# Four smaller pieces a bit in the selection, early block sums on VectorE, one weighted sum for the requests' index

## The chip, the cores and the metric

The kernel runs on one core of a Trainium2 chip. Its time is the device time of the whole program in microseconds. The kernel before took 1695.43 us, the median of three runs (1693.01 to 1697.52). All data are fp32.

## The reference

A trunk of two layers serves a prompt of 1024 tokens and eight later requests ("samples") of 16 tokens each, with caches of 512 tokens, with the same weights. Per layer: RMSNorm, one projection to the inputs of four branches of attention (A, B, C, M), the branches, each multiplied by silu of its own gate columns, and an output projection of 1024x1024 that is added to the stream. Branch A is the one that matters here: an indexer scores every key, and each query attends only to its top k.

```python
def dsa_attend(q, qi, wi, lim, k, v, ki, topk):
    L = k.shape[1]
    dots = jnp.einsum('bqhd,bld->bqhl', qi.astype(F32), ki.astype(F32)) * D_IDX ** -0.5
    score = jnp.einsum('bqh,bqhl->bql', wi.astype(F32) * H_IDX ** -0.5, jax.nn.relu(dots))
    admissible = jnp.arange(L)[None, :] < lim[:, None]
    score = jnp.where(admissible[None], score, -jnp.inf)
    top_s, top_i = lax.top_k(score, topk)
...
def merge(p, o_a, o_b, o_c, o_m, w_o):
    parts = [o.reshape(lead + (-1,)) * jax.nn.silu(p[g])
             for o, g in ((o_a, 'a_g'), (o_b, 'b_g'), (o_c, 'c_g'), (o_m, 'm_g'))]
    return jnp.concatenate(parts, axis=-1) @ w_o
```

## The kernel before, in words

**Order.** `program_order()` writes one list of steps for the whole program; every engine walks the list and does its own share of each step, in order, with semaphores between the engines. So the place of a step in the list is its place in each engine's queue. A tile is 128 tokens: eight of the prompt and a ninth (`ST_`) with the samples. The projection runs in chunks of 512 weight columns (A1, mm, B1, B2, C1, C2, M1, A2, then O0 and O1 for the output). A unit is one chunk for one tile: `project(c, t)` emits its matmuls in parts (`Pp`, then `P`), and between the parts the steps of an attention pack: `S` (scores on TensorE), `L` (logits on VectorE, exponentials on ACT), `T` (transposes), `Z` (the scaling of the gate), `V` (values, and the product with the gate on VectorE). A pack with several heads has two `L` and `T` halves; the second ones come from `odd_heads()`, just before the unit's `P`. TensorE writes scores to two buffers in psS, transposes to two in psT, and projections and values to two in psX.

**Selection.** The k-th largest score of each query is found bit by bit. VectorE keeps a threshold per strip (seven strips of 384 to 1024 scores, `thr`), and for each of 32 bits `count_below` counts the scores under the threshold (line 1572, one instruction and a read of its accumulator per strip); step `bit` updates the threshold from the counts (lines 1748 to 1758) and counts the strips `FIRST` (tiles 7, 6, 3), step `rest` the strips `REST` (samples, 5, 4, 2). Each ends in a drain. Then `equals`, `ranks` and `mask` make a mask of each strip. `select(time)` doles these steps out: it adds `time` to an account and emits steps, at planned costs, while the account is positive. A unit has two such places (four where two packs go through a unit, `two_packs`): at the start, and before `P`. All steps must be out before branch A's first pack.

**The requests' index.** For the samples, step `is` j scores a pair of requests (TensorE to psS, relu on ACT into one of two work buffers), and `iw` sums two such pairs over the heads with weights `wsel`: matmuls on line 1202 into a quarter of 32 rows per pair, then a copy and an addition on VectorE (lines 1736, 1737). `iw` 0 stands within the unit B1 `ST_`, `iw` 2 behind the unit B1 0, right before the first bit.

**Output projection.** It takes seven block products instead of eight (a Strassen scheme) per pair of tiles p and chunk: steps `G` c p n on TensorE (line 1142), each followed by additions to the stream on VectorE (line 1663, `ADDED_TO`) that free psX. The blocks need sums first: `Tw`, four sums of weight quarters of 128x1024 per chunk (line 1991), and `Sh`, four sums of rows of 128x512 per pair p (line 2008). All are made by GpSimd. `Tw` O0 and `Sh` 0 and 1 are emitted in one piece, four or eight at once, in the units of A2, when what they overwrite is free.

**Branch A's end.** In A2 units VectorE does the rotation of the queries (lines 1552 to 1558), the gate product (1652), the branch product (`V`, 1866) and, once, the product of the gathered samples with their gate (`R`, 1872), which frees a psT buffer.

Of the kernel before, what the change touches and what calls it, by code (L numbers as in the profile page):

```python
# [74 lines left out]
FIRST, REST = [NT - 1, NT - 2, 3], [ST_, 5, 4, 2]  # L75
# [67 lines left out]
def topk_steps():  # L143


    out = [(kind, i) for i in range(32) for kind in ("bit", "rest")]
    return out + [("bit", 32)] + [(kind, t) for t in [ST_] + SEL_TILES for kind in ("equals", "ranks", "mask")]


def program_order():  # L150
# [11 lines left out]
    queue = []  # L162

    def emit(*s, ahead=0):
# [3 lines left out]
    cost = lambda x: {"bit": 0.5 + count(FIRST) * (x[1] < 32), "rest": count(REST)}.get(  # L168
        x[0], {"equals": 1.9, "ranks": 2.2, "mask": 2.4}.get(x[0], 0) * STRIP_L.get(x[1], 0) / 960 + 0.5)
# [117 lines left out]
    for l in range(DEPTH):  # L287
# [54 lines left out]
        emit("iw", 0)  # L342
# [14 lines left out]
        units += [("M1", t) for t in [ST_] + TILES[:NT]] + [("A2", t) for t in A2_ORDER]  # L357
        for c, t in units:
# [252 lines left out]
def encoder(nc, d):  # L611
# [3 lines left out]
    with ExitStack() as ctx:  # L615
# [155 lines left out]
        n_work = {u: n for n, u in enumerate(steps("ip", "is"))}  # L771
        qs_ready = Signal(sem("qs_ready"), [(l, s) for l, s in order if s[0] == "is" or (s[0] == "S" and is_sample(s[1]))])
# [28 lines left out]
        rows_combined = Signal(sem("rows_combined"), events(["Sh"], lambda s: s[1:]))  # L801
        w_combined = Signal(sem("weights_combined"), events(["Tw"], lambda s: s[1:]))
# [21 lines left out]
        def row_sum(p, i):  # L824
# [7 lines left out]
                    (s4, upper[:, LAST_LINES, :], s2, ALU.subtract)][i]  # L832

# [184 lines left out]
        def _(pe):  # L1018
# [16 lines left out]
            for l, s in order:  # L1035
# [81 lines left out]
                elif k == "G":  # L1117
# [7 lines left out]
                    if (p, n) == (0, 2):  # L1125
                        pe.wait_ge(*w_combined.on((c, 3)))
                    if c == "O0" and n >= 3:
                        pe.wait_ge(*rows_combined.on((p, max(n - 3, 1))))
# [64 lines left out]
                elif k == "iw":  # L1193

                    both = [s[1], s[1] + 1]
                    for j in both:
# [3 lines left out]
                    for c0, c1 in ((0, PAST), (PAST, SKEYS)):  # L1200
                        for j in both:
                            mm = pe.matmul(S.ap(s)[32 * j:32 * j + 32, c0:c1], wsel[:, j, :],
                                           buf(n_work[l, ("is", j)] % 2)[:, c0:c1], start=True, stop=True)
# [138 lines left out]
        def _(act):  # L1342
# [4 lines left out]
            for l, s in order:  # L1347
# [135 lines left out]
                elif k in ("ip", "is"):  # L1483
# [3 lines left out]
                    if n >= 2:  # L1487
# [4 lines left out]
                        else:  # L1492
                            use = ("iw", pv[1] // 2 * 2)
                            act.wait_ge(*S.fill(use, pl).on(use, pl))
                    nc.scalar.activation(buf(n % 2)[:, 0:L], S.ap(s)[:, 0:L], ACT.Relu).then_inc(S.empty(s).sem, 1)  # L1495
# [37 lines left out]
        def _(dve):  # L1533
# [42 lines left out]
            for l, s in order:  # L1576
# [51 lines left out]
                elif k == "P" and (l, s[1:]) in worked.upto:  # L1628
# [24 lines left out]
                    dve.drain().then_inc(worked.sem, 1)  # L1653
                elif k == "G":
# [74 lines left out]
                elif k == "iw":  # L1729
                    j = s[1]  # L1730
                    dve.wait_ge(*S.fill(s).on(s))
                    if j == 0:
                        dve.wait_ge(*tmask.on("m"))
                    r0 = slice(32 * j, 32 * j + 64)
                    dst = sc[r0, SC_OFF[ST_]:SC_OFF[ST_] + SKEYS]
                    v.tensor_copy(dst[:, 0:PAST], S.ap(s)[r0, 0:PAST])
                    v.tensor_tensor(dst[:, PAST:SKEYS], S.ap(s)[r0, PAST:SKEYS], dst[:, PAST:SKEYS], ALU.add
                                    ).then_inc(S.empty(s).sem, 1)
                    dve.drain().then_inc(scored.sem, 1)
                elif k == "K" and s[1][0] == "bit":  # L1740
# [19 lines left out]
                    if i < 32:  # L1760
                        count_below(FIRST)
                        dve.drain()
                elif k == "K" and s[1][0] == "rest":
                    count_below(REST)
# [111 lines left out]
        def _(pool):  # L1876
# [89 lines left out]
            for l, s in order:  # L1966
# [9 lines left out]
                if k == "Tw":  # L1976

                    c, i = s[1:]
                    if i == 0:
                        pool.wait_ge(*w_loaded[chunks.index((l, c)) % 2].on(c))  # L1980
                        if c == "O0":
                            last_m = [q for ql, q in packs if ql == l and q[0] == "M"][-1]
                            for use in (("V", last_m), ("V", last_sample["A"])):
                                pool.wait_ge(*X.fill(use).on(use))
                        else:
                            pool.wait_ge(*logits.on((packs_of("A", 5)[-1], 1)))
                    t1, t2, t3, t4 = w_sums[c]
                    b11, b12 = [w_quarter(c, FIRST_LINES, h) for h in range(2)]
                    b21, b22 = [w_quarter(c, LAST_LINES, h) for h in range(2)]
                    out, a, b = [(t1, b12, b11), (t3, b22, b12), (t2, b22, t1), (t4, b21, t2)][i]  # L1990
                    g.tensor_tensor(out, a, b, ALU.subtract).then_inc(w_combined.sem, 1)
                    pool.drain()
                elif k == "Sh":

                    p, i = s[1:]
                    if i == 0:
                        if p >= 2:
                            use = ("G", "O1", p - 2, 6)
                            pool.wait_ge(*X.fill(use).on(use))
                        else:  # L2000
                            pool.wait_ge(*gated.on("A"))
                            pool.wait_ge(*k_stored.on("mm"))
                            pool.wait_ge(*v_stored.on(("mm", 1)))
                            pool.wait_ge(*sm_stored.on("s"))
# [4 lines left out]
                    pool.drain().then_inc(rows_combined.sem, 1)  # L2009
# [276 lines left out]
```

## Time and profile before

| | |
|---|---|
| median of three runs | 1695.43 us |
| profiled execution | 1695.91 us, its span 1694.1 us |
| TensorE matmul, weight load | 1657.6 us (98%), 1116.2 us (66%) |
| VectorE | 1083.6 us (64%) |
| ACT | 626.7 us (37%) |
| GpSimd | 321.7 us (19%) |
| mean granted clock of TensorE | 0.997 |

Shares are of the span. Both layers run the same steps, one layer behind the other. The views quoted below have, in their rows, the engine (PE is TensorE, DVE VectorE, POOL GpSimd), the line of the kernel and the operation. Engines overlap, so busy times don't add up to the span; a busy time of TensorE is modelled, with some overlap of neighbouring groups.

### The profile page before, as it was taken

The page shows a single profiled execution, that of the slowest core. Times are in us where ns is not written, and L with a number is a line of the kernel's source. Part 1 is how long each engine was busy: PE and PEld are TensorE (multiplying, and loading weights), DVE is VectorE, ACT ScalarE, POOL GpSimd, SP SyncE. Part 2 cuts the span into 40 slices and gives each one's busy share as a digit, 9 for nine tenths or more (in the row PEclk, how much of TensorE's full clock was granted, in tenths as well). Part 3 has the DMA queues.
Part 4 walks back from the last instruction along what each step waited for, and adds up shares of the span by engine and source line. Part 5 has one row for each costly group of instructions (what it writes and reads, how often), then busy time and mean ns, then how long its engine had stood idle before and what let it go on. Part 6 is the DMA issues. An engine that isn't in the chain of part 4 may idle for free.

```text
span 1694.1 us, 28367 instructions
## 1 busy us (share of the span) xinstructions
PE 1657.6 (98%) x9815; PEld 1116.2 (66%) x9815; DVE 1083.6 (64%) x2829; ACT 626.7 (37%) x1509; POOL 321.7 (19%) x500
## 2 busy tenths in 40 slices
PE   9999999999999999999999999999999999999998
PEld 4466666766677755588754666666666777556885
DVE  5747888788877334455445288887888773354454
ACT  3532334333343444422134323343333434445221
POOL 2242321100001022223021423220000010223110
PEclk9999999999999999999999999999999999999999
DMA  9343324123222341112251523241233132412021
GB/s 341 150 172 97 128 94 144 42 78 107 91 86 97 112 120 37 69 38 88 99 175 51 166 83 129 91 144 41 78 110 103 71 122 97 117 31 82 1 100 62
DMA packets 46382, 171.32 MB, mean 101 GB/s; under 512 B 11473, under 2 KB 11953, under 8 KB 43041
## 3 DMA queue, kind: packets, MB, share of 16 engines
q1 hardware_dynamic: 29632, 130.68, 22.8%
q0 software_dynamic: 16608, 38.83, 7.0%
q8 instruction: 80, 1.31, 0.3%
q14 instruction: 62, 0.50, 0.1%
HBM read 141.83 MB, written 30.73 MB: 102 GB/s over the span
## 4 chain that ended last, share of the span: by engine, by line
PE 63%; DVE 27%; issue 4%; ACT 3%; ACTq 1%; DVEq 1%; DMA 1%
PE psX L1113 32%; DVE lower L1572 15%; PE psX L1142 11%; PE psT L1026 6%; PE psX L1317 5%; PE psS L1250 4%; DVE work L1834 4%; PE psS L1169 2%; ACTq L1463 1%; DVE gate L1652 1%; PE psX L1026 1%; DVE work L1832 1%; ACT work L1504 1%; ACT gate L1377 1%; DVE gate L1848 1%
## 5 line engine op out<-in xcount | busy, mean ns | idle before, releaser
L1113 PE MATMUL psX<-wring,hT 128*128 128x512 f32 (+2 forms) x1504 | 609.5, 548 | 4.2 <-ACT qT L1423 2.6
L1113 PEld LDWEIGHTS psX<-wring,hT 128*128 128x128 f32 x1504 | 272.4, 191 | 222.4 <-issue 214.3
L1572 DVE TENSOR_SCALAR_CACHE_REDUCE lower<-sc,thr 128x640 uint8<-128x640 f32 (+5 forms) x462 | 407.3, 933 | 16.9 <-issue 9.0
L1113 PE MATMUL psX<-hT,wring 128*128 128x256 f32 (+1 forms) x1600 | 328.3, 359 | 4.5 <-ACT gate L1462 3.6
L1504 ACT ACTIVATE work<-work,stat 128x256 f32<-128x256 f32 (+7 forms) x288 | 200.0, 695 | 315.9 <-DVEq L1837 313.1
L1113 PEld LDWEIGHTS psX<-hT,wring 128*128 128x128 f32 x1600 | 274.2, 190 | 37.3 <-issue 8.2
L1513 ACT COPY work<-psT 128x512 f32<-128x512 f32 (+2 forms) x352 | 157.3, 488 | 295.2 <-PE psT L1026 292.8
L1026 PEld LDWEIGHTS psT<-con,work 128*128 128x128 f32 x1080 | 121.9, 141 | 77.0 <-issue 54.7
L1026 PE MATMUL psT<-con,work 128*128 128x128 f32 x1080 | 160.1, 279 | 10.9 <-DVE bias L1872 7.1
L1834 DVE CUSTOM_DVE_ANT_0 work<-psS,bias 128x640 f32<-128x640 f32 (+7 forms) x120 | 86.2, 718 | 39.1 <-issue 23.7
L1882 POOL DMA_DIRECT2D scratch_oscr<-gate x54 | 30.7, 569 | 346.2 <-DVEq L1868 294.3
L1834 DVE CUSTOM_DVE_ANT_0 work<-psS,sc 128x384 f32<-128x384 f32 (+5 forms) x48 | 42.8, 891 | 43.7 <-PE psT L1026 38.3
L1250 PE MATMUL psS<-kv,qT 64*128 64x512 f32 (+3 forms) x384 | 69.9, 482 | 0.0
L1317 PE MATMUL psX<-work,kv 128*64 128x128 f32 x1056 | 68.2, 277 | 0.0
L1317 PEld LDWEIGHTS psX<-work,kv 128*64 128x64 f32 x1056 | 56.7, 137 | 12.8 <-issue 12.3
L1495 ACT ACTIVATE work<-psS 128x640 f32<-128x640 f32 (+5 forms) x56 | 41.9, 748 | 61.2 <-PE psS L1191 28.2
L1142 PE MATMUL psX<-wring,hT 128*128 128x256 f32 x256 | 58.1, 380 | 0.0
L1663 DVE TENSOR_TENSOR kv<-psX,kv 128x256 f32<-128x256 f32 (+1 forms) x70 | 36.9, 535 | 32.5 <-PE psX L1142 31.7
L1663 DVE TENSOR_TENSOR xr<-psX,xr 128x256 f32<-128x256 f32 (+1 forms) x70 | 36.9, 535 | 30.7 <-PE psX L1142 29.9
L1866 DVE TENSOR_TENSOR gate<-psX,gate 128x256 f32<-128x256 f32 (+1 forms) x64 | 22.9, 358 | 50.0 <-ACTq L1521 41.7
L1504 ACT ACTIVATION_READ_ACCUMULATOR work<-work,stat 128x1 f32 x288 | 53.7, 187 | 0.0
L1552 DVE TENSOR_TENSOR lower<-stage,con 128x48 f32<-128x48 f32 (+1 forms) x36 | 10.8, 300 | 65.8 <-ACTq L1463 64.9
(272 smaller groups left out, 1953.8 us busy)
## 6 DMA issues: line engine op xcount, KB each, us to landing
wring<-in_w SPq DMA_DIRECT2D x16, 2048.0 KB, 8.5
cache<-in_kB SPq DMA_DIRECT2D x16, 512.0 KB, 6.1
cache<-in_vB SPq DMA_DIRECT2D x16, 512.0 KB, 4.0
cache<-in_kC SPq DMA_DIRECT2D x16, 512.0 KB, 6.1
cache<-in_vC SPq DMA_DIRECT2D x16, 512.0 KB, 4.8
scratch_oscr<-gate POOLq DMA_DIRECT2D x54, 128.0 KB, 2.0
hT<-scratch_oscr SPq DMA_DIRECT2D x18, 384.0 KB, 3.0
kv<-in_x SPq DMA_DIRECT2D x9, 512.0 KB, 6.1
```

The source lines that it names most:

```text
L1026: return pe.transpose(out, src, ident)
L1113: mm = pe.matmul(out, lhs, rhs, start=(kt == 0), stop=(kt == KT - 1))
L1142: mm = pe.matmul(X.ap(s)[:, 0:W], lhs[:, kt, :], rhs[:, kt, :], start=(kt == 0), stop=(kt == KT // 2 - 1))
L1169: mm = pe.matmul(S.ap(u)[:, c0:c1], qT[half, h // 2, t * P:(t + 1) * P], kA[half, 0, c0:c1], start=True, stop=True)
L1250: mm = pe.matmul(S.ap((s, hp))[:, at + c0:at + c1], q[half, :], keys[half, k0 + c0:k0 + c1], start=True, stop=True)
L1317: mm = pe.matmul(o[64 * hp:64 * hp + 64, i // 2 * P:(i // 2 + 1) * P], v, turned_buf(hp)[:, at:at + P], start=(b == 0), stop=(b == len(kb) ...
L1495: nc.scalar.activation(buf(n % 2)[:, 0:L], S.ap(s)[:, 0:L], ACT.Relu).then_inc(S.empty(s).sem, 1)
L1504: nc.scalar.activation(x, x, ACT.Exp, scale=-1.0, bias=stats(p)[:, 0, i:i + 1], accum_out=stats(p)[:, 1, i:i + 1]).then_inc(probs.sem, 1)
L1513: nc.scalar.copy(turned_buf(hp)[:, 512 * g:512 * g + w], T.ap(u)[:, 0:w]).then_inc(T.empty(u).sem, 1)
L1572: v.tensor_scalar(lower[:, at:at + STRIP_L[t]], sc[:, o], thr[:, n:n + 1], 0.0, ALU.is_lt, ALU.add, accum_out=below[:, n:n + 1])
L1663: last = v.tensor_tensor(x, X.ap(s)[:, 0:W].unsqueeze(1).to_broadcast([P, c1 - c0, W]), x, ALU.add)
L1834: last = v.tensor_tensor_reduce(dst, src, b_, -1.0, -NEG, ALU.add, ALU.min, nm)
```

## The change

It does three things. First, the counts of a bit go in four steps instead of two (`COUNTED`: tiles 7 and 2 with the update, then 6 and 3, then 5 and the samples, then 4), and `project` has four places for them in every unit, each worth a quarter of the pace: in a unit without two packs these are at the start, behind `operands()`, before `P`, and behind `P`. Second, `Tw` O0 and `Sh` 0 and 1 are VectorE's, and they are emitted from a list `sums`, two at a time at two places of a unit and one behind each `G` step. `Tw` O1 and `Sh` 2 and 3 stay on GpSimd; `Tw` O1 gets a wait more. Third, `iw` is one step for all four pairs, behind the unit B1 0; relu for pairs 2 and 3 writes into rows of `gate` instead of the work buffers, for which ACT waits for norm 10.

```diff
-FIRST, REST = [NT - 1, NT - 2, 3], [ST_, 5, 4, 2]
+COUNTED = [[7, 2], [6, 3], [5, ST_], [4]]
...
-    out = [(kind, i) for i in range(32) for kind in ("bit", "rest")]
+    out = [(kind, i) for i in range(32) for kind in ("bit", "second", "third", "fourth")]
...
+    sums = []
+
+    def add_sums(n):
+        for _ in range(n):
+            if sums:
+                emit(*sums.pop(0))
...
-        time = pace[0] / (4 if two_packs else 2)
+        time = pace[0] / 4
...
             odd_heads()
             select(time)
+            add_sums(2)
             emit("Pp", c, t, 3, 4)
...
             emit("Pp", c, t, 0, 2)
             operands()
+            select(time)
             emit("Pp", c, t, 2, 5)
         odd_heads()
         select(time)
+        add_sums(2)
         emit("P", c, t)
+        if not two_packs:
+            select(time)
...
-        emit("iw", 0)
...
-                emit("iw", 2)
+                emit("iw")
...
-                if c == "A2" and due and (l, (kind, at, 0)) not in o:
-                    for i in range(4):
-                        emit(kind, at, i)
+                if c == "A2" and due and (kind, at) not in begun:
+                    begun.append((kind, at))
+                    sums.extend((kind, at, i) for i in range(4))
...
             for n in range(7):
                 emit("G", c, p, n)
+                add_sums(1)
...
+            if s[0] == "is" and s[1] >= 2:
+                return gate[:, 4 * s[1] - 8:4 * s[1] - 4, :].rearrange("p a b -> p (a b)")
+            return buf(n_work[l, s] % 2)
...
-                    both = [s[1], s[1] + 1]
-                    for j in both:
+                    for j in range(PAIRS):
                         pe.wait_ge(*relued.on(("is", j)))
                     pe.wait_ge(*scored.on(("wsel",)))
                     scores_free(s)
                     for c0, c1 in ((0, PAST), (PAST, SKEYS)):
-                        for j in both:
+                        for j in range(PAIRS):
...
+                elif k == "Tw" and s[1] == "O0":
+
+                    c, i = s[1:]
+                    if i == 0:
+                        dve.wait_ge(*w_loaded[chunks.index((l, c)) % 2].on(c))
+                    v.tensor_tensor(*w_sum(c, i), ALU.subtract)
+                    dve.drain().then_inc(w_combined[True].sem, 1)
+                elif k == "Sh" and s[1] < 2:
+
+                    p, i = s[1:]
+                    if i == 0:
+                        dve.wait_ge(*k_stored.on("mm"))
+                        dve.wait_ge(*v_stored.on(("mm", 1)))
+                        dve.wait_ge(*sm_stored.on("s"))
+                        for t in (2 * p, 2 * p + 1):
+                            dve.wait_ge(*o_loaded[t].on("o"))
+                    v.tensor_tensor(*row_sum(p, i))
+                    dve.drain().then_inc(rows_combined[True].sem, 1)
...
-                    count_below(REST)
+                elif k == "K" and s[1][0] in ("second", "third", "fourth"):
+                    count_below(COUNTED[("second", "third", "fourth").index(s[1][0]) + 1])
                     dve.drain()
...
-                if k == "Tw":
+                if k == "Tw" and s[1] == "O1":
...
-                elif k == "Sh":
+                elif k == "Sh" and s[1] >= 2:
```

## Rows read from the trace of the kernel before

**Rows 1.** The page, busy time of each engine, share of the span, instructions

```profile
PE 1657.6 (98%) x9815; PEld 1116.2 (66%) x9815; DVE 1083.6 (64%) x2829; ACT 626.7 (37%) x1509; POOL 321.7 (19%) x500
```

**Rows 2.** TensorE's waits: for whom, total us, times, longest

```profile
PE psT L1026 <- DVE bias L1872: 7.1, 2, 3.5
...
PE psT L1026 <- DVE gate L1872: 3.3, 4, 1.3
```

**Rows 3.** Busy us by stretch: four with bit rounds, and one behind

```profile
sum 400.00, PE 392.23 PEld 265.53 DVE 346.51 ACT 141.62 POOL 73.33; mean PE 98.06 PEld 66.38 DVE 86.63 ACT 35.41 POOL 18.33
...
255.00:345.00 90.00, 90.00 (x564) 62.27 (x564) 71.16 (x179) 34.22 (x76) 12.97 (x24) 1.00 0.25 87
```

**Rows 4.** VectorE's waits from 150 to 255 us, first row

```profile
DVE work L1834 <- issue: 5.4, 22, 0.7
```

**Rows 5.** Busy us from 640 to 720 and from 1480 to 1560, sum

```profile
sum 160.00, PE 152.04 PEld 88.33 DVE 72.30 ACT 78.23 POOL 39.46; mean PE 76.02 PEld 44.16 DVE 36.15 ACT 39.12 POOL 19.73
```

**Rows 6.** The timeline, 673 to 680 us: start, us, engine, line, operation

```profile
673.36 2.35 POOL L1991 TENSOR_TENSOR qT<-wring,qT 128x1024 f32<-128x1024 f32 x1 [0.16 <-issue]
673.78 1.97 DVE L1552 TENSOR_TENSOR lower<-stage,con 128x32 f32<-128x32 f32 x1 [1.89 <-ACTq L1463]
...
675.87 2.40 POOL L1991 TENSOR_TENSOR cache<-wring,qT 128x1024 f32<-128x1024 f32 x1 [0.16 <-issue]
...
676.15 2.17 DVE L1557 TENSOR_TENSOR stage<-stage,lower 128x32 f32<-128x32 f32 x1
...
678.25 0.18 DVE L1558 TENSOR_TENSOR stage<-stage,lower 128x32 f32<-128x32 f32 x1
...
679.50 0.42 DVE L1872 TENSOR_TENSOR bias<-psT,bias 128x256 f32<-128x256 f32 x1
...
679.99 0.47 PE L1026 MATMUL psT<-con,work 128*128 128x128 f32 x1 [3.52 <-DVE bias L1872]
```

**Rows 7.** Two stretches of low granted clock (PEclk)

```profile
679.20:686.10 6.90, 6.12 (x11) 2.94 (x12) 2.75 (x6) 1.83 (x5) 5.07 (x4) 0.51 0.01 2
1522.30:1525.70 3.40, 3.40 (x9) 1.82 (x7) 1.55 (x3) 1.38 (x4) 3.04 (x3) 0.50 0.00 0
```

**Rows 8.** VectorE's groups by line and form: count | busy us, mean ns

```profile
L1663 DVE TENSOR_TENSOR xr<-psX,xr 128x512 f32<-128x512 f32 x30 | 20.4, 686 | 12.0 <-PE psX L1142 11.9
...
L1565 DVE TENSOR_TENSOR hT<-hT,con 128x1024 f32<-128x1024 f32 x9 | 11.0, 1225 | 10.0 <-DMA hT<-in_xT 6.0 <-DMA con<-in_const 3.1
```

**Rows 9.** The timeline, layer 1's first G steps

```profile
1560.96 2.36 POOL L1991 TENSOR_TENSOR cache<-wring 128x1024 f32<-128x1024 f32 x1 [27.52 <-DMA wring<-in_w]
...
1566.16 1.89 PE L1142 MATMUL psX<-cache,hT 128*128 128x256 f32 x8
```

**Rows 10.** The timeline: half an index sum, and matmuls on four quarters

```profile
132.24 1.27 PE L1202 MATMUL psS<-work,wsel 128*32 128x512 f32 x8
...
155.12 1.07 PE L1226 MATMUL psS<-cache,qs 128*32 128x512 f32 x8
...
156.00 0.40 PE L1231 MATMUL psS<-kv,qs 128*32 128x128 f32 x8
```

**Rows 11.** The timeline, 162 to 165 us: counts within and across steps

```profile
162.73 1.14 DVE L1572 TENSOR_SCALAR_CACHE_REDUCE lower<-sc,thr 128x896 uint8<-128x896 f32 x1
...
163.79 0.74 DVE L1572 TENSOR_SCALAR_CACHE_REDUCE lower<-sc,thr 128x512 uint8<-128x512 f32 x1
...
164.63 0.88 DVE L1572 TENSOR_SCALAR_CACHE_REDUCE lower<-sc,thr 128x640 uint8<-128x640 f32 x1
```

**Rows 12.** Line 1572 alone by stretch: busy us (xinstructions)

```profile
150.00:255.00 105.00, 61.75 (x140) 1.00 0.32 106
...
1192.00:1292.00 100.00, 58.59 (x132) 1.00 0.27 93
```

**Rows 13.** The timeline, 197 to 198.5 us

```profile
197.42 0.35 ACT L1458 COPY kv<-psX 128x256 f32<-128x256 f32 x1
...
198.48 1.75 PE L1113 MATMUL psX<-hT,wring 128*128 128x256 f32 x7 [1.12 <-ACT gate L1462]
```

More of the change, by code:

```diff
@@ L167, in program_order @@
     count = lambda part: sum(STRIP_L[t] / 960 + 0.25 for t in part)
-    cost = lambda x: {"bit": 0.5 + count(FIRST) * (x[1] < 32), "rest": count(REST)}.get(
-        x[0], {"equals": 1.9, "ranks": 2.2, "mask": 2.4}.get(x[0], 0) * STRIP_L.get(x[1], 0) / 960 + 0.5)
+    cost = lambda x: {"bit": 0.5 + count(COUNTED[0]) * (x[1] < 32), "second": count(COUNTED[1]), "third": count(COUNTED[2]),
+                      "fourth": count(COUNTED[3])}.get(x[0], {"equals": 1.9, "ranks": 2.2, "mask": 2.4}.get(x[0], 0) * STRIP_L.get(x[1], 0) / 960 + 0.5)
     def select(time):
@@ L800, in encoder @@
         o_loaded = [Signal(sem(f"branch_tile{t}_loaded"), each("o"), lambda e: 16) for t in TILES]
-        rows_combined = Signal(sem("rows_combined"), events(["Sh"], lambda s: s[1:]))
-        w_combined = Signal(sem("weights_combined"), events(["Tw"], lambda s: s[1:]))
+        early = lambda u: u[1][1] in ("O0", 0, 1)
+        sums_of = lambda kind, by_dve: [(l, s[1:]) for l, s in steps(kind) if early((l, s)) == by_dve]
+        rows_combined = {b: Signal(sem(f"rows_combined{int(b)}"), sums_of("Sh", b)) for b in (True, False)}
+        w_combined = {b: Signal(sem(f"weights_combined{int(b)}"), sums_of("Tw", b)) for b in (True, False)}
         res_added = Signal(sem("residual_added"), outs)
@@ L832, in row_sum, with w_sum @@
                     (s4, upper[:, LAST_LINES, :], s2, ALU.subtract)][i]
+        def w_sum(c, i):
+            t1, t2, t3, t4 = w_sums[c]
+            b11, b12 = [w_quarter(c, FIRST_LINES, h) for h in range(2)]
+            b21, b22 = [w_quarter(c, LAST_LINES, h) for h in range(2)]
+            return [(t1, b12, b11), (t3, b22, b12), (t2, b22, t1), (t4, b21, t2)][i]
         def w_quarter(c, rows_, half):
@@ L1200, in _ @@
                     for c0, c1 in ((0, PAST), (PAST, SKEYS)):
-                        for j in both:
+                        for j in range(PAIRS):
                             mm = pe.matmul(S.ap(s)[32 * j:32 * j + 32, c0:c1], wsel[:, j, :],
-                                           buf(n_work[l, ("is", j)] % 2)[:, c0:c1], start=True, stop=True)
+                                           index_buf(l, ("is", j))[:, c0:c1], start=True, stop=True)
                     mm.then_inc(S.fill(s).sem, 1)
@@ L1486, in _ @@
                     act.wait_ge(*S.fill(s).on(s))
-                    if n >= 2:
+                    if k == "is" and s[1] >= 2:
+                        act.wait_ge(*normed.on(10))
+                    elif n >= 2:
                         pl, pv = [x for x in n_work if n_work[x] == n - 2][0]
@@ L1492, in _ @@
                         else:
-                            use = ("iw", pv[1] // 2 * 2)
-                            act.wait_ge(*S.fill(use, pl).on(use, pl))
-                    nc.scalar.activation(buf(n % 2)[:, 0:L], S.ap(s)[:, 0:L], ACT.Relu).then_inc(S.empty(s).sem, 1)
+                            act.wait_ge(*S.fill(("iw",), pl).on(("iw",), pl))
+                    nc.scalar.activation(index_buf(l, s)[:, 0:L], S.ap(s)[:, 0:L], ACT.Relu).then_inc(S.empty(s).sem, 1)
                     act.drain().then_inc(relued.sem, 1)
@@ L1760, in _ @@
                     if i < 32:
-                        count_below(FIRST)
+                        count_below(COUNTED[0])
                         dve.drain()
-                elif k == "K" and s[1][0] == "rest":
-                    count_below(REST)
+                elif k == "K" and s[1][0] in ("second", "third", "fourth"):
+                    count_below(COUNTED[("second", "third", "fourth").index(s[1][0]) + 1])
                     dve.drain()
@@ L1980, in _ @@
                         pool.wait_ge(*w_loaded[chunks.index((l, c)) % 2].on(c))
[L1981 to L1991, printed above, removed]
+                        pool.wait_ge(*X.fill(("V", last_sample["A"])).on(("V", last_sample["A"])))
+                        pool.wait_ge(*logits.on((packs_of("A", 5)[-1], 1)))
+                    g.tensor_tensor(*w_sum(c, i), ALU.subtract).then_inc(w_combined[False].sem, 1)
                     pool.drain()
-                elif k == "Sh":
+                elif k == "Sh" and s[1] >= 2:
                     p, i = s[1:]
                     if i == 0:
[L1997 to L2004, printed above, removed]
+                        use = ("G", "O1", p - 2, 6)
+                        pool.wait_ge(*X.fill(use).on(use))
                         for t in (2 * p, 2 * p + 1):
@@ L2008, in _ @@
                     g.tensor_tensor(*row_sum(p, i))
-                    pool.drain().then_inc(rows_combined.sem, 1)
+                    pool.drain().then_inc(rows_combined[False].sem, 1)
                 elif k == "G" and s[3] == 6:
```

17 lines of the change are left out of this document (8 added, 9 removed).

## The prediction

> **What bounds the kernel now.** I read the page first: the reader is to see TensorE busy for 98% of the span and VectorE for 64% [rows 1]. A busy TensorE can hide stalls, so next come the waits by engine. The longest in TensorE's list are two waits of 3.5 us, 7.1 us together, for line 1872 on VectorE, the product of branch A's sample rows with their gate [rows 2]. Then the stages: in four stretches of 95 to 105 us, where the bit rounds of the selection lie beside attention, TensorE is busy for 392.2 of 400 us and VectorE for 346.5 [rows 3]. In the first of them the head of VectorE's list of waits is its own issue: it never waits for data [rows 4]. So two engines run at nearly one rate there, and what is added to VectorE can reach TensorE. Elsewhere VectorE has room: it is busy for 72.3 of 160 us in the two stages where branch A meets the output projection [rows 5]. TensorE bounds the kernel; a change pays where it takes a stall or work from TensorE.
>
> **Part 1: the early sums move from GpSimd to VectorE.** Before, GpSimd makes four sums of 1024 columns (2.35 and 2.40 us in the rows) for O0 and eight of 512 for row pairs 0 and 1, per layer. The timeline shows what they do to VectorE. The rotation products of 128x32 on lines 1552 and 1557, like the one on line 1558 at 0.18 us, take 1.97 and 2.17 us, and each of the two ends when a GpSimd sum ends (675.75 beside 675.71; 678.32 beside 678.27). The two slow ones stand before line 1872 in VectorE's queue; it starts at 679.50, and TensorE's next transpose at 679.99, after 3.52 us idle [rows 6]. Without the two delays (1.79 + 1.99 = 3.8 us) line 1872 would start near 675.7, and the idle would end where it began, at 676.5. I take it as gone in both layers: -7.0 us.
> At this gap the granted clock falls: 0.51 for 6.9 us from 679.2, and 0.50 for 3.4 us from 1522.3, where the same wait ends in the second layer [rows 7]. That is 1.2 GHz instead of 2.4, right behind TensorE's longest idle time. Half of both is lost: (6.9 + 3.4) / 2 = 5.1 us. With the gap gone I take it as kept: -5.1 us (0 if the clock falls all the same).
> The sums cost VectorE 4 x 1.22 + 8 x 0.69 = 10.4 us a layer, by its products of 1024 and additions of 512 columns [rows 8]. Eight of a layer's twelve stand, two at a time, in the units A2 6 and 7, where VectorE is idle more than half the time [rows 5]; a pair of 1.22 delays a branch product by at most 2.6 us ahead of idle of that size: zero. If that cover were gone, up to 10.4 us a layer would be paid.
> The other four, of row pair 1, now stand behind the first four G steps. In layer 1 GpSimd's four sums for O1 run there one behind the other, the first from 1560.96 and 2.36 us long, so for some 9.5 us [rows 9]. The moved sums have both inputs in SBUF, as the slow products of [rows 6] have, so each but the first may wait for up to 2.35 us, and the additions that free psX queue behind. TensorE has two psX halves and 1.9 us of work a step [rows 9], so a good part is hidden: 0 to 7 us, I take +2.5, nearer the hidden end.
> The Trainium skill has the cause: SBUF — State Buffer, "SBUF: two separate sides", says that VectorE with two SBUF inputs and GpSimd take a shared port pair exclusively, for the whole instruction. It speaks for the -7.0 and against the G steps of layer 1; by it that collision could be the full 7, and the sum 4.5 us later.
>
> **Part 2: one weighted sum.** Each half of the requests' index takes TensorE 1.27 us: four matmuls of 512 and four of 128 columns, on two of four column quarters. Eight matmuls of 512 on all four quarters take 0.88 us (155.12 to 156.00) and eight of 128 take 0.40 [rows 10], so all four pairs fit into the time of one half. One half a layer goes, 1.2 us with the overlap: -2.4 us (0 at worst: a matmul group is not longer than before). VectorE saves a copy and an addition a layer. Relu for pairs 2 and 3 writes into gate rows; the wait added to ACT there is for a norm long done, and behind it nothing is late. The selection begins where it did.
>
> **Part 3: four pieces a bit.** The seven strips and the planned pace stay. A unit has four places instead of two, but places one and two have nothing of VectorE's between them, so ahead of a unit's second logits pass stand on average the same counts as before. New is that the unit's gate product (line 1652) comes before the last piece, and that pieces end at finer steps. Each piece ends in a drain. Inside a piece the count of 512 follows the start of that of 896 by 1.06 us (1.14 long); at its end the next piece's count follows the start of the 512 by 0.84 us (0.74 long) [rows 11]. A boundary costs 0.10 + 0.08 = 0.18 us. There are two more a bit: 32 x 2 x 2 = 128, 23 us of VectorE. Each bit shows as 14 instructions of line 1572 (seven counts, seven reads); the four stretches hold 531, from 140 in the first to 132 in the last [rows 12], 38 bits: 13.7 us where VectorE never waits.
> How much reaches TensorE? It waited 8.2 us in these stretches, ten rows of the kind shown, 0.6 to 1.1 us each as a rule. In that one ACT can't empty psX until its exponentials are through, and they wait for VectorE's logits, behind three counts; TensorE stands 1.12 us [rows 13]. Best, finer pieces take all 8.2 away; worst, all 23 pass. Behind a stretch VectorE has room again, busy for 71.2 of 90 us from 255 [rows 3], so a growing lag may be carried out of it. I take 7 passing and 5 of the waits gained: +2.
> The Trainium skill, VectorE: DVE Perf Modes, "The DRAIN you can't avoid", says that a flush stands behind each operation anyway and a semaphore adds nothing; by it the split would be free and only the gain of 5 would stand. The 0.18 us of the rows speaks against it for an explicit drain behind a count.
>
> **Sum,** against the profiled execution's 1695.9 us (span 1694.1 and 1.8 around it): 1695.9 - 7.0 - 5.1 + 2.5 - 2.4 + 2 = 1685.9. The median of the runs shown is 0.5 lower, 1695.4, so I forecast 1685.5. A difference under 0.3% (5 us) can't be told from none.
>
> **Rivals.** (a) The split is free or a gain: 6 of TensorE's 8.2 us of waits go and the collision is hidden: 1695.4 - 14.5 - 6 = 1675 (1672 to 1679). For it: the waits are short against a piece; against: the boundary's 0.18.
> (b) The gap stays under another name: line 1872 is still behind a rotation and a branch product, half the gap and half the lost clock remain: 1695.4 - 6 - 2.4 + 4.5 = 1691.5. For it: TensorE waits for line 1872 in four other places, 3.3 us [rows 2]; against: delays of 3.8 us fill the 3.5.
> (c) The split doesn't do what it says, because places one and two adjoin on VectorE: finer pieces win none of the waits and cost the 7: 1695.4 - 12.1 - 2.4 + 2.5 + 7 = 1690.4.
> (d) Slower: the boundaries. If VectorE is the true bound wherever bits are counted, all 23 us reach TensorE: 1695.4 - 14.5 + 23 = 1704. It turns the change to a loss from 14.5/128 = 0.11 us passed on per boundary. Against it: VectorE's room behind the stretches.
>
> **Chances.** Forecast 0.56 (its own range 1680 to 1690), (a) 0.16, (b) 0.10, (c) 0.10, (d) 0.08. Faster by over 0.3%: the first two and a third of (b) and (c), 0.78; within: 0.14; slower: 0.08. The range leaves out the low end of (a) and most of (d): 1675 to 1694.
>
> **What would show it.** TensorE's wait for line 1872 at the end of branch A gone in both layers, the clock 1.00 there, lines 1552 and 1557 never over 0.5 us: part 1. In layer 1's first G steps TensorE waiting for line 1663, and a moved sum of over 1 us: the collision. Two groups on line 1202 instead of four: part 2. TensorE's waits in the four stretches, 8.2 before, about 10 after: part 3. I am wrong if that stands at under 4 or over 20, or if the clock falls elsewhere.

## The result, and the profile after

The changed kernel takes 1721.2 us (median of 4 runs, 1720.7 to 1723.4) beside 1696.0 us for the kernel before on the same chip: ratio 1.0152, 95% interval 1.0140 to 1.0164. It is 25 us slower, where the forecast was 10 us faster; the time lies outside the range and beyond the slower rival's 1704.

The page of the changed kernel first: busy time of each engine, beside [rows 1].

```profile
PE 1661.1 (96%) x9815; PEld 1116.2 (65%) x9815; DVE 1103.4 (64%) x2849; ACT 625.1 (36%) x1509; POOL 281.9 (16%) x476
```

TensorE is busy for 3.5 us more in a span that is 27.5 us longer (1721.6 against 1694.1), so nearly all of the loss is waiting. TensorE's waits over the whole span (for whom, total, times, longest) say on whom:

```profile
PE psX L1053 <- ACTq L1542: 18.2, 14, 2.5
PE psX L1140 <- ACT kv L1451: 8.2, 4, 2.9
PE psT L1053 <- DVE gate L1914: 7.8, 4, 2.3
...
PE psX L1140 <- DMA wring<-in_w: 3.0, 2, 1.9
```

The first row of [rows 2], 7.1 us for the sample rows' product of branch A, is gone. In its place stands ScalarE: it copies the transposes out of psT late (up to line 1542) and empties psX late (line 1451). In the stretches of the selection the waits are these (133 to 600 us, then 975 to 1440 us):

```profile
PE psX L1053 <- ACTq L1542: 8.1, 5, 2.5
PE psX L1140 <- ACT kv L1451: 4.0, 2, 2.5
PE psT L1053 <- DVE gate L1914: 3.9, 2, 2.3
PE psX L1140 <- ACT qT L1449: 2.8, 2, 1.5
PE psX L1140 <- ACT gate L1456: 0.4, 1, 0.4
PE psX L1140 <- ACT gate L1488: 0.4, 1, 0.4
...
PE psX L1053 <- ACTq L1542: 8.2, 5, 2.5
PE psX L1140 <- ACT kv L1451: 4.2, 2, 2.9
```

With the rows left out they sum to 19.6 + 19.6 = 39.2 us; the same view of the kernel before sums to 7.3 + 6.7 = 14.0. In the four stretches of [rows 3], each moved by the lag of its work, the 8.2 us of the forecast are about 19 (4.8, 5.8, 2.9 and 5.7), so its sign of being wrong, over 20, did not quite show; the larger part of the growth lies outside them. ScalarE is busy for a third of the span, so it is late because it is itself held up. VectorE's waits in the changed kernel show by what:

```profile
DVE lower L1579 <- ACTq L1489: 57.6, 30, 6.8
DVE gate L1679 <- ACTq L1489: 54.2, 25, 9.5
```

Line 1679 is the gate product of step P (1652 before), and line 1489 the end of ScalarE's copies and gates out of psX. Before, VectorE waited 31.5 us there, 16 of them in two waits of 8 ahead of the selection, which stay. So VectorE waits for ScalarE's work on psX, and ScalarE, in order too, waits for VectorE's logits. The experiments below take this apart.

The granted clock, as in [rows 7], by windows (the column ahead of the last two):

```profile
117.00:120.40 3.40, 3.40 (x5) 1.35 (x4) 3.28 (x3) 0.00 (x0) 0.00 (x0) 0.51 0.06 25
181.90:185.30 3.40, 3.40 (x5) 1.32 (x6) 2.41 (x6) 0.41 (x1) 2.92 (x6) 0.50 0.94 320
543.70:547.10 3.40, 3.40 (x25) 2.24 (x20) 0.59 (x2) 0.37 (x1) 0.60 (x1) 0.50 0.02 5
1035.20:1038.60 3.40, 3.40 (x6) 1.34 (x5) 2.63 (x8) 0.82 (x2) 3.06 (x6) 0.51 0.68 247
1397.10:1400.50 3.40, 3.40 (x16) 2.34 (x13) 1.02 (x4) 0.74 (x2) 0.60 (x1) 0.50 0.11 39
```

The two places of before run at the full 2.4 GHz; instead there are five stretches at 1.2 GHz, each close behind an idle time of TensorE of 1.9 to 2.9 us. TensorE is busy throughout, so half of 17.0 us is lost, 8.5, against 4.8 before (half of the 9.5 us busy in [rows 7]). This sign of being wrong, the clock falling elsewhere, did show.

The end of branch A, on VectorE's timeline, beside [rows 6]:

```profile
693.13 0.19 DVE L1584 TENSOR_TENSOR stage<-stage,lower 128x32 f32<-128x32 f32 x1
693.24 0.19 DVE L1585 TENSOR_TENSOR stage<-stage,lower 128x32 f32<-128x32 f32 x1
...
694.51 0.42 DVE L1914 TENSOR_TENSOR bias<-psT,bias 128x256 f32<-128x256 f32 x1
```

The rotation step that took 2.17 us takes 0.19, and the product comes 1.4 us behind it. This part of the forecast holds.

Where the time went follows from when the same products start in the two traces. In each layer the lag grows by 16.1 and 16.8 us during the selection (32.9). Of that the added waits are 39.2 - 14.0 = 25.2, and four of the five slow stretches 6.8. It falls by 5.9 and 4.3 us at the end of branch A, falls by 1.3 in each layer where half of the index sum is gone, and grows by 1.9 and 0.9 right behind that, by 1.8 for the first slow stretch, and by 1.8 in layer 1's G steps. With 0.5 us at the start that is 32.9 - 10.2 - 2.6 + 2.8 + 1.8 + 1.8 + 0.5 = 27.0 of the 27.5 us.

### The profile page after: what moved, and what is told of

It reads as the page before. It is cut to its first block, busy times and chain, and to the rows that moved or that the text cites. A ratio compares the mean times of both kernels' runs of the same rounds, so it can differ in the third digit from the quotient of the medians.

```text
span 1721.6 us, 28477 instructions
## 1 busy us (share of the span) xinstructions
PE 1661.1 (96%) x9815; PEld 1116.2 (65%) x9815; DVE 1103.4 (64%) x2849; ACT 625.1 (36%) x1509; POOL 281.9 (16%) x476
## 4 chain that ended last, share of the span: by engine, by line
PE 57%; DVE 30%; issue 5%; ACT 3%; ACTq 2%; DVEq 2%; DMA 1%
PE psX L1140 30%; DVE lower L1599 16%; PE psX L1169 10%; PE psT L1053 5%; DVE work L1876 5%; PE psX L1343 4%; PE psS L1276 4%; PE psS L1196 2%; ACTq L1489 1%; DMA wring<-in_w 1%; ACT work L1531 1%; DVE gate L1679 1%; PE psX L1053 1%; DVE gate L1890 1%; ACT gate L1403 1%
## 5 line engine op out<-in xcount | busy, mean ns | idle before, releaser
L1599 DVE TENSOR_SCALAR_CACHE_REDUCE lower<-sc,thr 128x640 uint8<-128x640 f32 (+5 forms) x462 | 417.4, 935 | 33.8 <-issue 16.5
L1053 PE MATMUL psT<-con,work 128*128 128x128 f32 x1080 | 159.8, 279 | 10.1 <-DVE gate L1914 7.8
L1679 DVE SCALAR_TENSOR_TENSOR gate<-stage,gate 128x256 f32<-128x256 f32 (+1 forms) x46 | 21.7, 472 | 55.9 <-ACTq L1489 54.2
L1874 DVE TENSOR_SCALAR_CACHE_REDUCE work<-psS 128x256 f32<-128x256 f32 x72 | 30.6, 425 | 35.2 <-PE psT L1053 25.0
```

The source lines that it names most:

```text
L1053: return pe.transpose(out, src, ident)
L1599: v.tensor_scalar(lower[:, at:at + STRIP_L[t]], sc[:, o], thr[:, n:n + 1], 0.0, ALU.is_lt, ALU.add, accum_out=below[:, n:n + 1])
L1679: v.scalar_tensor_tensor(out=ga, in0=th, scalar=1.0, in1=ga, op0=ALU.add, op1=ALU.mult)
```

## The experiments

**One part at a time.** Part 3 alone, on the kernel before:

```diff
-FIRST, REST = [NT - 1, NT - 2, 3], [ST_, 5, 4, 2]
+COUNTED = [[7, 2], [6, 3], [5, ST_], [4]]
...
-        time = pace[0] / (4 if two_packs else 2)
+        time = pace[0] / 4
...
             operands()
+            select(time)
             emit("Pp", c, t, 2, 5)
...
         emit("P", c, t)
+        if not two_packs:
+            select(time)
```

> The kernel before with part 3 alone: four pieces a bit at four places. The recorded forecast's steps give +2 us (7 passing, 5 of waits gained), its rival of boundaries at most +23. Theory 1 (each added boundary costs VectorE about 0.24 us and all of it reaches TensorE) and theory 2 (the places put bit and second piece ahead of the second logits pass) together: about +33 us, ratio 1.019, with TensorE waiting over 8 us for the evacuation of psX in the V packs. If this stands under +10, the loss of the changed kernel is an interaction with the moved sums.

It is 35.0 us slower (1731.2 against 1696.2; ratio 1.0209, 1.0193 to 1.0224), near the 33 of the two theories together. The loss is part 3's own. Part 1 alone, with this as its core:

```diff
+                elif k == "Tw" and s[1] == "O0":
+                    ...
+                    v.tensor_tensor(*w_sum(c, i), ALU.subtract)
+                    dve.drain().then_inc(w_combined[True].sem, 1)
+                elif k == "Sh" and s[1] < 2:
+                    ...
+                    v.tensor_tensor(*row_sum(p, i))
```

> The kernel before with part 1 alone: the early sums on VectorE, two pieces a bit. The recorded forecast's steps give -7.0 - 5.1 + 2.5 = -9.6 us, with the clock at 1.00 at the end of branch A and waits for line 1663 in layer 1's first G steps. The two traces' offsets give -6.4 in layer 0 and -4.3 in layer 1, +1.8 for the collision, and the lost clock kept: about -9 to -12. If it is within 3 us of before, the gain was handed back by something the offsets hide.

It is 6.5 us faster (1689.7; 0.9960, 0.9947 to 0.9973), less than the 9 to 12 expected. Between the traces the end of branch A gives 5.7 and 4.6 us, and layer 1's G steps take 1.9 back; 1.7 us are lost before the first branch product, where the two kernels do the same: up to there the executions of the several kernels lie from 1.0 us ahead of the kernel before to 1.6 behind it. Parts 1 and 2 together, the counts as before:

```diff
-        emit("iw", 0)
...
-                emit("iw", 2)
+                emit("iw")
```

> Parts 1 and 2 together, the counts as before. The recorded forecast's steps give -7.0 - 5.1 + 2.5 - 2.4 = -12 us, 1684. The offsets between the traces of before and after give for part 2 a gain of 1.2 us a layer, and behind it a wait for the next weight block's DMA (1.9 and 0.9 us) and a half clock of 3.4 us in the first layer: about 0 to +1 in all, so 1688 to 1690 by them.

It is 6.3 us faster (1689.2 against 1695.5; 0.9968, 0.9954 to 0.9983), as part 1 alone: part 2 brings no gain that the runs can tell. The timeline of this kernel shows it, where TensorE comes 1.2 us earlier to the next weight block:

```profile
114.92 2.84 PE L1136 MATMUL psX<-wring,hT 128*128 128x512 f32 x6 [1.36 <-DMA wring<-in_w]
```

With part 1 alone it starts at 114.75 in the trace of that kernel with one drain less, without a wait. The sum saved only brings TensorE to a transfer that has not landed: its waits for the weight blocks are 2.6 us in two places, against 0.3 with part 1 alone, and the sum saved is 2.4.

**Part 3 in two: pieces, and places.** Four pieces at the two old places, then two pieces at the four new places (each is one half of the first diff above):

> The kernel before with four pieces a bit, but still two places in every unit, so two more drains a bit (128 in all). Theory 1 (boundaries): nearly the whole of part 3's loss, +20 to +30 us. Theory 2 (placement): under +8. The recorded forecast's price (0.18 us a boundary, 7 of 23 passing): +2 to +7.

> The kernel before with two pieces a bit, but four places in every unit, each worth a quarter of the pace: no more drains than before, only other positions for the steps. Theory 1: no loss, within 3 us. Theory 2: most of part 3's loss, +15 or more, with waits of TensorE for the evacuation of psX by ScalarE.

The pieces cost 12.7 us (1708.9; 1.0075, 1.0060 to 1.0090), the places 27.6 (1723.8; 1.0170, 1.0153 to 1.0188). The pieces' loss lies between the 20 to 30 of theory 1 and the 2 to 7 of the forecast's price. Theory 1 (boundaries are the loss) fails as the main cause, and my guess in the forecast that the places do no harm fails outright. Theory 2 has the size, but not the reason: by the program order the counts ahead of a unit's second logits pass are of 2432 scores a query in each of the 21 units that have such a pass in the selection, in the kernel before and with the four places alike. First the pieces: VectorE's count group with four pieces, then with four places but two pieces (busy, mean ns, idle before).

```profile
L1573 DVE TENSOR_SCALAR_CACHE_REDUCE lower<-sc,thr 128x640 uint8<-128x640 f32 (+5 forms) x462 | 417.4, 935 | 32.5 <-issue 16.6
```

```profile
L1575 DVE TENSOR_SCALAR_CACHE_REDUCE lower<-sc,thr 128x640 uint8<-128x640 f32 (+5 forms) x462 | 407.3, 933 | 17.2 <-issue 7.9
```

The kernel before has 407.3 and 16.9. So 128 boundaries cost VectorE 10.1 + 15.6 = 25.7 us, 0.20 each. That half of it reaches the end is not shown, because the pieces also regroup the strips. Ahead of the second logits pass, where 2432 scores a query stood in each unit, there are now from 1408 to 3456 (2444 on average). In an early unit with 2816 (four counts instead of three) TensorE waits 2.64 us for ScalarE to empty psX, and a slow stretch follows. VectorE is 1.2 us later there than in the kernel before at the first logits pass and 1.9 at the second (TensorE was 0.6 us ahead of it until then), so the boundaries so far and the larger counts both have a share. TensorE's lag grows by 4.2 us there, and by 3.9 in the same unit of layer 1, 1.3 and 0.9 of which are given back. That is 5.9 of the 12.7 us in two units, and TensorE's waits for this copy (line 1451 of the changed kernel) are 7.2 us with the pieces alone, 1.4 before and 1.4 with the places alone. What the drains and what the regrouping cost was not separated. Then the places: VectorE's waits with two pieces at four places.

```profile
DVE gate L1655 <- ACTq L1466: 66.8, 30, 8.2
```

31.5 us have become 66.8. One of them on that kernel's timeline, VectorE and ScalarE:

```profile
1095.07 0.83 DVE L1837 CUSTOM_DVE_ANT_0 work<-psS,bias 128x640 f32<-128x640 f32 x1 [0.18 <-issue]
...
1097.79 0.42 DVE L1655 SCALAR_TENSOR_TENSOR gate<-stage,gate 128x256 f32<-128x256 f32 x1 [1.89 <-ACTq L1466]
1098.35 0.88 DVE L1575 TENSOR_SCALAR_CACHE_REDUCE lower<-sc,thr 128x640 uint8<-128x640 f32 x1
```

```profile
1095.98 0.83 ACT L1507 ACTIVATE work<-work,stat 128x640 f32<-128x640 f32 x1 [4.01 <-DVEq L1840]
...
1096.81 0.35 ACT L1461 COPY kv<-psX 128x256 f32<-128x256 f32 x1
1097.06 0.38 ACT L1464 ACTIVATE stage<-psX 128x256 f32<-128x256 f32 x1
1097.34 0.38 ACT L1465 ACTIVATE gate<-psX 128x256 f32<-128x256 f32 x1
```

The same unit in the kernel before, VectorE and then ScalarE's last copy out of psX:

```profile
1080.42 0.82 DVE L1834 CUSTOM_DVE_ANT_0 work<-psS,bias 128x640 f32<-128x640 f32 x1 [0.18 <-issue]
...
1081.40 0.88 DVE L1572 TENSOR_SCALAR_CACHE_REDUCE lower<-sc,thr 128x640 uint8<-128x640 f32 x1 [0.15 <-issue]
...
1083.94 0.61 DVE L1572 TENSOR_SCALAR_CACHE_REDUCE lower<-sc,thr 128x384 uint8<-128x384 f32 x1
...
1084.64 0.43 DVE L1652 SCALAR_TENSOR_TENSOR gate<-stage,gate 128x256 f32<-128x256 f32 x1
```

```profile
1082.69 0.39 ACT L1462 ACTIVATE gate<-psX 128x256 f32<-128x256 f32 x1
```

The second logits pass (1095.07) releases ScalarE's exponentials (1095.98), behind them ScalarE empties psX (1096.81 to 1097.72), and only then the gate product of P can run (1097.79). In the kernel before the `rest` counts stand between the logits and P (1081.40 to 1084.55) and fill this time: ScalarE is through at 1083.08, and P starts without a wait. With the fourth place they stand behind P: VectorE idles for 1.89 us and then counts for 3.2 us ahead of this unit's branch product and the next unit's logits. From 1074 to 1160 us this idle time is 0.4 us before and 7.9 us here, and TensorE's lag grows by 5.6 us from 1053 to 1155 us of the kernel before (13.3 to 18.9). The planner's program order tells how often: behind P stand 2 of a layer's 64 steps with counts before, 14 of 64 here (15 with the last update of the threshold), and 29 of 128 in the changed kernel.

**Is it the fourth place?** The place added behind `operands()` against the one behind P, each alone, two pieces a bit:

```diff
-        time = pace[0] / (4 if two_packs else 2)
+        time = pace[0] / 4
         select(time)
...
             operands()
+            select(time)
...
-        select(time)
+        select(time if two_packs else 2 * time)
         emit("P", c, t)
```

> The kernel before with two pieces a bit and three places in a unit: the second place is there, the fourth (behind the unit's gate product P) is not. The first four runs gave a new theory 3: VectorE, which works in order, meets P before counts that stood ahead of it, and sits idle until ScalarE has emptied the unit's last projection (its waits for ScalarE at the gate product 31.5 us before, 66.8 with the four places). Theory 3: no loss here, within 3 us, and that wait stays near 31. Theory 2 in its first form (counts ahead of the second logits pass): ten steps of each layer move from the first place to the second, with nothing of VectorE's between, so it too gives no change; what it can't give is a gain. If this loses over 8 us, theory 3 isn't the cause of the 27.6.

```diff
         odd_heads()
-        select(time)
+        select(time if two_packs else time / 2)
         emit("P", c, t)
+        if not two_packs:
+            select(time / 2)
```

> The kernel before with two pieces a bit, the second place left out and the fourth kept (weights 1/2, 1/8, 1/8 and 1/4). Behind P stand 15 steps a layer, as with all four places (2 before). Theory 3: the whole loss of the four places, +22 to +30 us, with VectorE waiting 60 us or more for ScalarE at the gate product. Rival (the second place harms): within 5 us of before.

The second of these edits gives half of the pace to the first place, a quarter to the one before P and a quarter to the one behind it; the weights that its expectation names are not those of the edit. Without the fourth place the time is that of before (1696.0 against 1696.4; 0.9997, 0.9988 to 1.0006). With it and not the second the whole loss is there (1723.6; 1.0159, 1.0144 to 1.0174). VectorE's wait in the one and in the other:

```profile
DVE gate L1653 <- ACTq L1464: 31.5, 15, 8.2
```

```profile
DVE gate L1654 <- ACTq L1465: 65.9, 29, 7.9
```

And the changed kernel itself without its fourth place, whose share of the pace goes to the third:

```diff
-        select(time)
+        select(time if two_packs else 2 * time)
         add_sums(2)
         emit("P", c, t)
-        if not two_packs:
-            select(time)
```

> The changed kernel with one edit undone: no fourth place behind the unit's gate product, its share of the pace goes to the third; four pieces a bit and parts 1 and 2 stay. Theory 3: the loss of the fourth place goes (places_134 lost 27.2 us and pieces and places together 35.0 where the pieces alone lost 12.7, so 22 to 27): 1721.2 - 22 to 27 = 1694 to 1699, and VectorE's wait for ScalarE at the gate product falls from 54 to about 30 us. If the four pieces themselves were the loss (the recorded rival of the boundaries), it stays over 1712.

It takes 1700.8 us, 20.4 below the changed kernel (1.0026 of before, 1.0014 to 1.0037), a little less than the 22 to 27 expected; VectorE's wait falls to 31.1 us:

```profile
DVE gate L1677 <- ACTq L1487: 31.1, 12, 9.5
```

What is left above 1689.2, the kernel with parts 1 and 2 alone, is 11.5 us for the pieces, as the 12.7 above. So of the waits in the changed kernel's first list those for line 1542 belong mainly to the fourth place (18.2 us, 6.2 without it) and those for line 1451 to the pieces (8.2 and 8.3).

**Is VectorE's time worth the same the other way?** The threshold update flips a constant bit behind the shift; it can as well be flipped beside the comparison, which saves a drain a bit from the second bit on, 30 a layer and 60 in all (the expectations say 62):

```diff
                         v.tensor_tensor(over[:, :], below[:, :], con[:, C_LEFT:C_LEFT + len(STRIPS)], ALU.is_gt)
+                        if 1 < i and b > 0:
+                            v.tensor_scalar(bits, bits, 1 << (b - 1), None, ALU.bitwise_xor)
                         dve.drain()
...
-                        if b > 0:
+                        if b > 0 and i == 1:
                             dve.drain()
```

> The kernel before with one drain less a bit (62 in all): the constant bit is flipped beside the comparison instead of behind the shift, so one of the threshold update's three boundaries is gone. A boundary in such a chain is 0.08 us (0.17 long, the next one starts 0.25 later). The rows of the four pieces say that of 25.6 us more of VectorE's time 12.7 reached the end, one half. So 62 x 0.08 = 5 us less of VectorE's time and -2.5 us of the whole; if a drain costs more than the rows show, up to -6. If VectorE's time is one-sided (added time costs, removed time brings nothing), 0.

> Part 1 alone (the early sums on VectorE) with one drain less a bit as well. If the two add up: -6.5 - 2.5 = -9 us, 1687. If the drains bring nothing: 1689.7 as part 1 alone.

It is 6.3 us faster (1690.1 against 1696.4; 0.9963, 0.9949 to 0.9977), just beyond the most that I expected. The update on this kernel's timeline:

```profile
1091.53 0.17 DVE L1748 TENSOR_TENSOR over<-below,con 128x7 int32<-128x7 f32 x1
1091.61 0.16 DVE L1750 TENSOR_SCALAR thr<-thr 128x7 int32<-128x7 int32 x1
1091.86 0.17 DVE L1756 SCALAR_TENSOR_TENSOR thr<-over,thr 128x7 int32<-128x7 int32 x1
1092.12 1.28 DVE L1572 TENSOR_SCALAR_CACHE_REDUCE lower<-sc,thr 128x1024 uint8<-128x1024 f32 x1
```

From the comparison to the first count it takes 0.59 us; in the kernel before it takes 0.76 (1098.71 to 1099.47 on its timeline). The flip starts 0.08 us behind the comparison with no drain between, while the shift behind a drain starts 0.25 later: my 0.08 a boundary took only the gap and left out that two operations with no drain between overlap. 0.17 x 60 = 10.2 us of VectorE bring 6.3. The slow clock may have a share in this: the profiled execution, 2.4 us faster than the median, has 3.4 us at 1.2 GHz where the kernel before has 10.2. With part 1 it is 14.1 us faster than before (1682.3; 0.9917, 0.9904 to 0.9931), more than the 9 expected, about the sum of the two gains measured, and the best version of all. Neither trace with part 1, with these drains or without, has such a stretch ahead of the last 10 us, so the 7.4 us between them (1689.7 to 1682.3) are not the clock's.

> Parts 1 and 2 with the drain of the threshold update taken out as well: 14.1 us below before without part 2. If part 2 brings its 1.2 us a layer: 1680. If the weight block's DMA takes it back: 1682 to 1684.

With part 2 on top: 1683.4 us (0.9925, 0.9911 to 0.9938), as expected if the transfer takes the gain back; part 2 brings nothing there either.

**The moved sums beside the G steps.** In the best version, the last four sums ahead of the first G step:

```diff
+            add_sums(len(sums))
             for n in range(7):
                 emit("G", c, p, n)
-                add_sums(1)
```

> Part 1 with one drain less a bit, and the last four sums (row pair 1) all ahead of the first G step instead of one behind each of four steps. In layer 1 one of them took 2.37 us beside GpSimd's sums, and the G steps were 1.9 us later than before. Ahead of the steps, where GpSimd is idle, each takes 0.69 us: that 1.9 us goes, against up to 4 x 0.8 us by which the first step's additions are late, with two halves of psX to cover them: -1 to -2 us against 1682.3. If the additions are the tighter thing: +1 to +3.

I missed with this one: 1689.6 us (0.9962, 0.9950 to 0.9975), 7.3 above the best version. Its timeline, VectorE and then TensorE:

```profile
1545.23 0.69 DVE L1695 TENSOR_TENSOR sc<-hT 128x512 f32<-128x512 f32 x1 [0.33 <-issue]
1546.05 0.69 DVE L1695 TENSOR_TENSOR lower<-sc,hT 128x512 f32<-128x512 f32 x1
1546.86 0.69 DVE L1695 TENSOR_TENSOR hT<-hT 128x512 f32<-128x512 f32 x1
1547.67 2.75 DVE L1695 TENSOR_TENSOR om<-hT,lower 128x512 f32<-128x512 f32 x1
1550.62 1.21 DVE L1706 TENSOR_TENSOR kv<-psX,kv 128x256 f32<-128x256 f32 x2 [0.19 <-issue]
```

```profile
1551.19 3.75 PE L1166 MATMUL psX<-cache,hT 128*128 128x256 f32 x8 [4.52 <-DVE kv L1706]
```

The collision is not gone, only moved to the fourth sum, and all four now delay the first addition: TensorE stands for 4.52 us, and its next eight matmuls take 3.75 us where [rows 9] has 1.89, because the granted clock is 0.50 from 1548.9 to 1555.7. TensorE is busy for 4.5 of these 6.8 us, so 2.3 of the loss are the clock's. In layer 0 no sum is slow, and TensorE still stands 2.81 us behind the four sums. One sum a step, as in the change, is the better order.

## Why the prediction was wrong

**What bounds the kernel:** right. TensorE bounds it, and in the selection VectorE's time reaches it, in both directions.

**Part 1** (-7.0 - 5.1 + 2.5): the mechanism was right, and the sizes of its first two terms were near. The gap goes in both layers, the clock is full there, and lines 1552 and 1557 never take over 0.5 us. In the trace with part 1 alone the lag falls by 3.7 us in each layer at the gap (7.4 for 7.0) and by 3.0 and 1.6 in what were the slow stretches (4.6 for 5.1; TensorE was still idle for the first 0.8 us of layer 0's). What was left out comes right behind: TensorE's next transpose waits 1.11 us for ScalarE where it waited 0.28, in both layers, and the ends of branch A give 10.3 us together instead of 12.1. The collision in layer 1 is there as forecast: one moved sum takes 2.28 us beside a sum of GpSimd's, and TensorE then waits for line 1708 (1663 before). The changed kernel's timeline:

```profile
1586.45 2.36 POOL L2025 TENSOR_TENSOR cache<-wring 128x1024 f32<-128x1024 f32 x1 [76.73 <-DMA wring<-in_w]
1587.07 2.28 DVE L1697 TENSOR_TENSOR lower<-sc,hT 128x512 f32<-128x512 f32 x1
...
1594.99 1.97 PE L1169 MATMUL psX<-wring,bias 128*128 128x256 f32 x8 [1.05 <-DVE xr L1708]
```

It cost 1.8 us for a forecast of 2.5. The other three moved sums took 0.69 us. One came before GpSimd's first and one in a gap of 3.1 us between GpSimd's first two; the third started together with GpSimd's second (1591.93), and there it was GpSimd's that took 2.91 us instead of 2.36. So GpSimd's sums did not stand one behind the other as in [rows 9], and the full 7 us that the Trainium skill's port rule (SBUF — State Buffer, "SBUF: two separate sides") allowed did not come. The rule itself agrees with the slow products here: the moved sum that took 2.28 us started 0.62 us behind GpSimd's and ended 0.54 us after it.

**Part 2** (-2.4): the 1.2 us a layer go from TensorE's work, and two groups stand where four did. What was late next was left out of the forecast: the next weight block, whose DMA ends when it did before. The step had "0 at worst", and 0 it was, but by luck: the reason given for that bound was the length of a matmul group, not a transfer.

**Part 3** (+2) is the step that failed, in two terms. The larger is the sentence that ahead of the second logits pass stand on average the same counts. For the places that is so in every unit, and it is beside the point: I looked at what stands ahead of the logits and named as new only that "the unit's gate product comes before the last piece". I priced that at nothing. But VectorE works in order, and the counts were the cover of the gate product's wait for ScalarE. Moved behind P they cost twice: the wait is paid idle, and the branch product and the next logits come later. It measured 27.6 us with two pieces and 20.4 in the changed kernel. The smaller term is the price of the pieces: 0.18 us a boundary was near (0.20), but the pieces cost 12.7 us, not 7 less 5 of waits gained. Here the words "on average" hid something: per unit the counts ahead of the logits are no longer even, and the longest new wait stands where they grew. No wait was gained: the selection's waits grew from 14.0 to 39.2 us.

**The rivals.** (a) is out by the sign, and (b), because the gap did go. (d) had the sign and the engine, with the wrong carrier: the pieces bring 12.7 us where it had 23 for their boundaries, and the rest is the order of the steps. It put the bound at "all boundaries pass", and a cost that lies outside the boundaries was no part of any case. (c) saw that the second place does nothing, which the kernel with three places confirms (0.4 us), and stopped one place short. The Trainium skill's sentence that a flush stands behind each operation anyway (VectorE: DVE Perf Modes, "The DRAIN you can't avoid") does not carry over to an explicit drain here: operations with none between them overlap by about 0.1 us, and each drain taken out brought VectorE 0.17 us.

**Open.** 35.0 us for part 3 alone is less than 12.7 + 27.6, and part 3 on top of parts 1 and 2 is 32.0 (1721.2 - 1689.2). The traces show where the difference lies: with four pieces the fourth place adds less to VectorE's wait at the gate product, 21.3 us (29.7 to 51.0) where it adds 35.3 with two, and costs 35.0 - 12.7 = 22.3 us instead of 27.6. Why it adds less was not tried. The slow clock is part of each of these sums. Ahead of the last 10 us the profiled executions have 10.2 us at 1.2 GHz before, 13.7 with the pieces, 23.9 with the places, 23.9 with both and 17.1 in the changed kernel, so half of the growth, 1.7, 6.8, 6.8 and 3.4 us, is the most that it explains of each loss; the waits that it follows were not varied apart from it.

## What to carry to other kernels

On an engine that works in order, filler work has a place that it protects: the wait right behind it. Before it is moved past an instruction, ask what that instruction waits for and whether the filler was what hid it. And an average of what stands ahead of a step hides the units in which it grew. Where two engines run at nearly one rate, saved drains on the second one can reach the end: an independent operation set beside another, ahead of the same drain, took 60 drains out and brought 6.3 us for one line moved.

## What the runs showed of the hardware

- An explicit drain between two 128x7 operations on VectorE costs 0.17 us: 0.25 us from start to start with it, 0.08 without.
- In the changed kernel five idle times of TensorE of 1.9 to 2.9 us were each followed by 3.4 us at 1.2 GHz, and two of 2.33 and 2.35 us (at 262.2 and 1115.1) were not. In the kernel with one drain less a bit the wait of 3.53 us for line 1874 (1872 before) stands in both layers, and only in layer 1 did a slow stretch follow (1513.6). So the length of an idle time alone does not tell whether the clock falls.
- A 128x512 sum on VectorE that started behind a sum of GpSimd's took 2.28 to 2.75 us, and 0.69 alone; started together with one, it took 0.69 and GpSimd's 2.91 instead of 2.36.
